# A transformer pair on one core: attention probabilities scaled on GpSimd before their transposes

## The reference, cut to what matters

```python
# first block: o_s and o_w, gated per head
p_s = jax.nn.softmax(jnp.where(dist_s >= 0, s_s, NEG_INF), axis=-1)
o_s = jnp.einsum('bgjtm,bgtmd->btgjd', p_s.astype(vsg.dtype), vsg)
...
o = g[..., 0:1] * o_c + g[..., 1:2] * o_s + g[..., 2:3] * o_w
# even layer
p = jax.nn.softmax(sc, axis=-1).astype(v.dtype)
return jnp.einsum('bkgqs,bskd->bqkgd', p, v)
...
oa = oa * jax.nn.silu(ga)
# odd layer
m = jnp.maximum(jnp.max(sc, axis=-1, keepdims=True), sink_l)
p = jnp.exp(sc - m)
denom = jnp.sum(p, axis=-1, keepdims=True) + jnp.exp(sink_l - m)
o = jnp.einsum('bnkgqs,bnskd->bnqkgd', (p / denom).astype(v.dtype), vb)
```

## Time and profile before

| | us |
|---|---|
| three runs | 1368.05, 1366.27, 1367.89 |
| median | 1367.89 |
| profiled execution | 1367.87 |
| its span, first to last instruction | 1365.3 |
| PE busy | 1316.9 (96%) |
| DVE busy | 820.5 (60%) |
| ACT busy | 440.2 (32%) |
| POOL busy | 637.6 (47%) |
| mean granted clock of PE | 0.987 |

### The profile page before, as it was taken

One profiled execution on the slowest core, in us unless ns is written; L12 is line 12 of the kernel. 1 busy time (PEld: TensorE's weight loads), 2 busy tenths in 40 slices (PEclk: granted clock), 3 DMA queues, 4 the chain that ended last, 5 costly groups with the idle time before them and its releaser, 6 DMA issues. The chain is left out here.

```text
span 1365.3 us, 19690 instructions
## 1 busy us (share of the span) xinstructions
PE 1316.9 (96%) x7254; PEld 1036.5 (76%) x7254; DVE 820.5 (60%) x1586; ACT 440.2 (32%) x948; POOL 637.6 (47%) x523
## 2 busy tenths in 40 slices
PE   7999999999999999999999999999999999999996
PEld 5897766688888888888788788876556788767675
DVE  4898689914554777777572456535655254156643
ACT  4201455523122112222110332255656122244521
POOL 5865222246676666666576365532000365622230
PEclk9999999999999999999999989999999999999998
DMA  5622110112343455555543124211000123211111
GB/s 177 239 68 77 32 41 24 46 62 83 103 169 123 169 187 200 199 186 191 178 155 95 44 93 152 88 47 32 0 1 1 62 83 93 93 38 41 32 47 62
DMA packets 37522, 130.24 MB, mean 95 GB/s; under 512 B 4544, under 2 KB 4800, under 8 KB 37184
## 3 DMA queue, kind: packets, MB, share of 16 engines
q1 hardware_dynamic: 26640, 93.11, 21.3%
q10 hardware_dynamic: 10800, 35.98, 7.1%
HBM read 126.98 MB, written 2.10 MB: 95 GB/s over the span
## 5 line engine op out<-in xcount | busy, mean ns | idle before, releaser
L1044 POOL TENSOR_TENSOR wlo<-raw,whi 128x1024 fp32r<-128x1024 f32 x171 | 417.0, 2438 | 14.3
L1040 POOL TENSOR_TENSOR whi<-raw,ones 128x2 fp32r<-128x2 f32 x171 | 40.9, 239 | 677.5 <-DMA raw<-in_w 677.5
L461 PE MATMUL bank<-ysplit,whi 128*128 128x512 f32 x984 | 314.5, 398 | 2.1 <-DVE xbuf L2254 2.1
L461 PE MATMUL bank<-hhi,whi 128*128 128x512 f32 x536 | 218.1, 407 | 0.4 <-DVE arena L2164 0.4
L461 PEld LDWEIGHTS bank<-ysplit,whi 128*128 128x128 f32 x984 | 184.4, 190 | 38.9 <-issue 3.2
L461 PE MATMUL bank<-hhi,wlo 128*128 128x512 f32 x536 | 209.9, 392 | 0.0
L461 PE MATMUL bank<-hlo,whi 128*128 128x512 f32 x536 | 209.4, 391 | 0.0
L461 PE MATMUL bank<-ysplit,wlo 128*128 128x512 f32 x496 | 194.9, 393 | 0.0
L1041 POOL TENSOR_SCALAR whi<-raw 128x1022 fp32r<-128x1022 f32 x171 | 185.8, 1086 | 0.0
L461 PEld LDWEIGHTS bank<-hhi,whi 128*128 128x128 f32 x536 | 100.9, 188 | 25.6 <-issue 6.6
L461 PEld LDWEIGHTS bank<-hhi,wlo 128*128 128x128 f32 x536 | 100.9, 188 | 22.0
(11 more groups left out here) (315 smaller groups left out, 2100.5 us busy)
## 6 DMA issues: line engine op xcount, KB each, us to landing
raw<-in_w SPq DMA_DIRECT2D x171, 512.0 KB, 3.6
arena<-in_ada ACTq DMA_DIRECT2D x48, 512.0 KB, 4.3
xbuf<-in_xT ACTq DMA_DIRECT2D x12, 256.0 KB, 5.6
xbuf<-in_w ACTq DMA_DIRECT2D x1, 2048.0 KB, 8.9
first<-in_w ACTq DMA_DIRECT2D x1, 2048.0 KB, 8.4
out_t<-xbuf SPq DMA_DIRECT2D x8, 256.0 KB, 2.2
xbuf<-in_xT SPq DMA_DIRECT2D x4, 256.0 KB, 6.4
first<-in_uq ACTq DMA_DIRECT2D x1, 768.0 KB, 6.5
```

What stands on the lines that cost most here:

```text
L461: m = mm(b[:, :], w[:, s, k * P:(k + 1) * P], x, start=(k == 0 and part == 0), stop=(k == DC - 1 and part == 2))
L1040: g.tensor_tensor(whi[:, s, 0:2], raw[:, s, 0:2], ones[:, :], ALU.mult)
L1044: g.tensor_tensor(wlo[:, s, :], raw[:, s, :], whi[:, s, :].bitcast(F32), ALU.subtract)\
```

## The change

Four things, in the words of the code:

1. Each step's two row sums are inverted at once by DVE (`inverse_sums`, one reciprocal of 128x2 per step). POOL multiplies the step's exps by them in place, half by half (`n_norm`, `ab_norm`, `c_norm`; in N by the gate as well), and PE's transposes wait for that (`p_norm`). All spreads are gone, with the multiplications by them. In N both branches of a head pair add up in one bank, and one addition per head pair takes it out with the compressed branch.
2. POOL's loop is written out: `splits` for whole stretches, and inside the attentions one part of a split (`split_part`: the high half, then two halves of the low one) behind a step's products.
3. In C the sink stands as one more column beside the scores (written by POOL, `c_sink`), so that the exp sums it; its own exp and sums are gone.
4. In AB and C ACT's copies of the transposes of step i-2 come ahead of the exps of step i. The down projection begins with banks 2, 3, 7 of its first two rows, and the wait for the modulation product stands ahead of bank 4; of the last four rows banks 0 and 1 of the first three come ahead of the wait for the last split. Even output units 3 to 7 use `EOUT_REST`.

```diff
@@ -178,7 +178,7 @@
...
-EOUT_BANKS = (0, 1, 2)
+EOUT_BANKS, EOUT_REST = (0, 1, 2), (3, 0, 1, 2)
...
@@ -352,13 +351,11 @@
...
-        p3 = area(3 * 2 * 3 * P).rearrange("p (s h n) -> p s h n", s=3, h=2)
+        p3 = area(3 * 2 * (3 * P + 1)).rearrange("p (s h n) -> p s h n", s=3, h=2)
...
@@ -572,7 +575,7 @@
...
-                    pe.wait_ge(*p_ready.at(("N", s, half)))
+                    pe.wait_ge(*p_norm.at(("N", s, half)))
...
@@ -582,26 +585,16 @@
...
-                if qt == 0:
-                    bank.take(pe, N_O, ("O", "N", s // TT))
-                b = bank.tiles[found[("bank", ("O", "N", s // TT))]]
+                if qt == 0 and br == 0:
+                    bank.take(pe, N_O, ("O", "N", i))
+                b = bank.tiles[found[("bank", ("O", "N", i))]]
...
                                vtok[:, kt, br * P + half * HD:br * P + half * HD + HD],
-                               npt[:, s % 2, half, kt * P:(kt + 1) * P], start=(kt == 0), stop=(kt == qt),
+                               npt[:, s % 2, half, kt * P:(kt + 1) * P], start=(br == 0 and qt == 0 and kt == 0), stop=(br == 1 and kt == qt),
...
-            def n_spread(p):
-                pe.wait_ge(*dve_did.at(("N", "rinv", p)))
-                b = bank.take(pe, C_R, ("N", "R", p))
-                for qt in range(TT):
-                    for half in range(2):
-                        x = n_col(p, half, qt)
-                        m = mm(b[64 * half:64 * half + 64, qt * P:(qt + 1) * P],
-                               rinv[:, x:x + 1].to_broadcast([P, HD]), ident[:, :], start=True, stop=True)
-                m.then_inc(*pe_did.up(("N", "R", p)))
...
@@ -762,17 +753,27 @@
...
-            pe.wait_ge(*dve_did.at(("ada", ADA_UP - 1)))
-            for i in range(FC):
-                u = UNIT[("down", i)]
-                pe.wait_ge(w_split.sem, u + 1)
+
+            def down_rows(i):
+                pe.wait_ge(w_split.sem, UNIT[("down", i)] + 1)
                 pe.wait_ge(*dve_did.at(("fa", i)))
-                for n in (2, 3, 6, 7, 4, 5, 1, 0) if i < LATE else ():
-                    if i == 0:
-                        bank.take(pe, (n,), ("down", n))
+
+            for part in (2, 3, 7), (6, 4, 5, 1, 0):
+                for i in range(2):
+                    down_rows(i)
+                    for n in part:
+                        if n == 4 and i == 0:
+                            pe.wait_ge(*dve_did.at(("ada", ADA_UP - 1)))
+                        if i == 0:
+                            bank.take(pe, (n,), ("down", n))
+                        m = down_block(i, n)
+                    if n == 0:
+                        m.then_inc(*unit_done.up(UNIT[("down", i)]))
+            for i in range(2, LATE):
+                down_rows(i)
+                for n in (2, 3, 7, 6, 4, 5, 1, 0):
                     m = down_block(i, n)
-                if i < LATE:
-                    m.then_inc(*unit_done.up(u))
+                m.then_inc(*unit_done.up(UNIT[("down", i)]))
...
@@ -784,8 +785,13 @@
...
+            for i in range(LATE, FC - 1):
+                down_rows(i)
+                for n in range(2):
+                    down_block(i, n)
+            down_rows(FC - 1)
             for n in range(DC):
-                for i in range(LATE, FC):
+                for i in range(LATE if n >= 2 else FC - 1, FC):
...
@@ -936,7 +930,7 @@
...
-                unit("eout", i, src=e_parts)
+                unit("eout", i, src=e_parts, pool=EOUT_REST)
...
@@ -1044,13 +1026,88 @@
...
+            def split_part(u, part):
+
+                s = u % WS
+                if part == 0:
+                    pool.wait_ge(landed[s].sem, u // WS * 16 + 16)
+                    g.tensor_tensor(whi[:, s, 0:2], raw[:, s, 0:2], ones[:, :], ALU.mult)
+                    g.tensor_scalar(whi[:, s, 2:D], raw[:, s, 2:D], 1.0, 1.0, ALU.mult, ALU.mult).then_inc(w_hi.sem, 1)
+                    return
+                at = slice((part - 1) * D // 2, part * D // 2)
+                pool.wait_ge(w_hi.sem, u + 1)
+                m = g.tensor_tensor(wlo[:, s, at], raw[:, s, at], whi[:, s, at].bitcast(F32), ALU.subtract)
+                if part == 2:
+                    m.then_inc(w_split.sem, 1)
...
+            def n_norm(s):
+                i, b, qt = n_steps[s]
+                L = (qt + 1) * P
+                pool.wait_ge(*dve_did.at(("N", "rinv", s)))
+                for half in range(2):
+                    x, gate = n_col(s // TT, half, qt), 3 * (i + 4 * half) + 1 + b
+                    g.tensor_scalar(np_[:, s % 3, half, 0:L], np_[:, s % 3, half, 0:L], rinv[:, x:x + 1],
+                                    gate3[:, qt, gate:gate + 1], ALU.mult, ALU.mult).then_inc(*p_norm.up(("N", s, half)))
...
+            def ab_norm(s):
+                p, qt = ab_steps[s]
+                pool.wait_ge(*dve_did.at(("AB", "rinv", s)))
+                for half in range(2):
+                    x = n_col(p, half, qt)
+                    g.tensor_scalar(abp[:, s % 3, half, :], abp[:, s % 3, half, :], rinv[:, x:x + 1], 1.0,
+                                    ALU.mult, ALU.mult).then_inc(*p_norm.up(("AB", s, half)))
...
+            first = UNIT[("q", 3)] + WS
+            splits(0, first)
+            pool.wait_ge(*dve_did.at(("qlo", 3)))
+            for i in range(len(n_steps)):
+                n_norm(i)
+                if i % TT:
+                    split_part(first + i // TT, i % TT - 1)
+            first, end = first + len(n_steps) // TT, UNIT[("ega", 2)] + WS
+            splits(first, end)
+            for i in range(len(ab_steps)):
+                ab_norm(i)
+                if 2 <= i < 20:
+                    split_part(end + (i - 2) // 3, (i - 2) % 3)
+            first, end = end + 6, UNIT[("og", 0)] + WS
+            splits(first, end)
+            pool.wait_ge(*dve_did.at("nsink"))
+            for i in range(3):
+                c_sink(i)
+            for i in range(len(c_steps)):
+                c_norm(i)
+                if i + 3 < len(c_steps):
+                    c_sink(i + 3)
+                if i % TT:
+                    split_part(end + i // TT, i % TT - 1)
+            splits(end + len(c_steps) // TT, NU)
...
@@ -1464,10 +1512,10 @@
...
+                if 2 <= i < n + 2:
+                    ab_copy(i - 2)
                 if i < n:
                     ab_exp(i)
-                if 2 <= i < n + 2:
-                    ab_copy(i - 2)
...
@@ -1506,16 +1554,16 @@
...
-                    A(p3[:, i % 3, half, 0:w], p3[:, i % 3, half, 0:w], ACT.Exp, bias=nmax[:, x:x + 1],
+                    act.wait_ge(*pool_did.at(("C", "sink", i)))
+                    A(p3c(i, half, 1), p3c(i, half, 1), ACT.Exp, bias=nmax[:, x:x + 1],
...
@@ -1531,15 +1579,10 @@
...
+                if 2 <= i < n + 2:
+                    c_copy(i - 2)
                 if i < n:
                     c_exp(i)
-                if 2 <= i < n + 2:
-                    c_copy(i - 2)
...
@@ -1834,28 +1877,18 @@
...
-            def n_rinv(p):
-                i, b = p // 2, p % 2
-                x = n_col(p, 0, 0)
-                dve.wait_ge(*p_ready.at(("N", p * TT + TT - 1, 1)))
-                link(V.reciprocal(rinv[:, x:x + 8], rsum[:, x:x + 8]))
-                r = rinv[:, x:x + 8].rearrange("p (t h) -> p t h", t=TT)
-                V.tensor_tensor(r, r, gate3[:, :, 3 * i + 1 + b:24:12], ALU.mult).then_inc(*dve_did.up(("N", "rinv", p)))
-
-            def n_out(p):
-                i, b = p // 2, p % 2
-                dve.wait_ge(*act_did.at(("N", "R", p)))
-                dve.wait_ge(*pv_done.at(("N", p * TT + TT - 1)))
-                dst = nacc(i) if b == 0 else hs[:, 0, :]
-                V.tensor_tensor(dst, bank.of(("O", "N", p))[:, :], nspread, ALU.mult).then_inc(*dve_did.up(("N", "t", p)))
-                bank.freed(("O", "N", p), dve_did, ("N", "t", p))
-                if b:
-                    dve.wait_ge(*dve_did.at(("N", "t", p)))
-                    link(V.tensor_tensor(nacc(i), nacc(i), hs[:, 0, :], ALU.add))
-
-            def n_add_cmp(i):
+            def inverse_sums(name, s, x):
+
+                dve.wait_ge(*p_ready.at((name, s, 1)))
+                V.reciprocal(rinv[:, x:x + 2], rsum[:, x:x + 2]).then_inc(*dve_did.up((name, "rinv", s)))
+
+            def n_out(i):
+
                 dve.wait_ge(*act_did.at(("cmp", "o", i)))
-                V.tensor_tensor(nacc(i), nacc(i), ncmp(i), ALU.add).then_inc(*dve_did.up(("N", "o", i)))
+                dve.wait_ge(*pv_done.at(("N", 8 * i + 7)))
+                V.tensor_tensor(nacc(i), bank.of(("O", "N", i))[:, :], ncmp(i), ALU.add)\
+                    .then_inc(*dve_did.up(("N", "o", i)))
...
@@ -2208,18 +2239,11 @@
...
-                dve.wait_ge(*pe_did.at(("AB", "R", p)))
                 dve.wait_ge(*dve_did.at(("g", "ega", p) if p < 4 else ("g", "egb", p - 4)))
-                if p:
-                    dve.wait_ge(*dve_did.at(("AB", "y", p - 1)))
```

(6 more changed lines are left out.)

134 lines of the change are left out of this document (44 added, 90 removed).

## The result

The changed kernel takes 1353.77 us (median of five runs, 1352.43 to 1357.61) against 1368.05 for the kernel before beside it; the ratio is 0.9897, with a 95% interval of 0.9879 to 0.9915. It is faster by 14 us where 24 were forecast: inside the range (1328 to 1363) and on the right side, but 10 us short of the likeliest value and just outside the forecast's own case (1336 to 1352). One of the five executions of the kernel before took 2616.91 us and is left out of the ratio. The profiled execution is the one of 1352.43 us, with a span of 1350.4.

The account below looks back on a forecast made before the run. PE was taken to bound the kernel nearly everywhere, DVE the second part of N. Terms N, AB, C, down stage, even outputs: 1367.9 + 6 - 12.5 - 6.0 - 8.7 - 2.9 = 1343.8 us; range 1328 to 1363.

Parts of the forecast that it names:

- N: First block's attention: -2 us in its first part, +8 in the second, where DVE sets the pace; +6 in all.
- C: Second block's third attention: -8.2 us for spreads (small PE products), +2 cover, -2.3 end, +2.5 start; -6.0 in all.
- AB: Second block's first two attentions: spreads give 7.8 us, most waits for ACT's copies go, products stay hidden; -12.5.
- the forecast's own case: Whole kernel: time falls within 1336 to 1352 us; chance 0.55.
- rival 3: N costs more: transposes wait for POOL's products too; +10 to +18 us there, total 1354 to 1362; chance 0.14.
- Down stage and even outputs: Down projection and even output units: new order and banks remove PE's gaps and slow clock; -8.7 and -2.9 us.
- Rival 4: Down stage: mended waits only move; 11.6 us of gains shrink to 2, total about 1354; chance 0.06.
- DVE reads PSUM in nearly all it does here: AB: step behind counting POOL's products as hidden, with 1.1 us to spare; the stage's forecast was -12.5 us.
- Who comes second waits to the end of the other's instruction: N: DVE's taps and POOL's instructions exclude each other; 20 pairs of products cost DVE 20 us.
- The waits at the end (2.1) go: End of C: the output no longer needs a spread; -2.3 us with the smaller waits beside them.
- Rival 1: N: products cost DVE nothing, so the stage follows PE; -12 us instead of +6, total 1326; chance 0.13.
- Rival 2: AB's bare steps and all N: pointer-scalar product costs 1.22 us (total 1361) to 1.5 (1380) for 512; chance 0.12.

## Why the prediction came out as it did

The time came out inside the range, but in part by luck: AB, C and C's start gave 12.3 us less than counted, and what hides it is the width of the range and 2.4 us less cost in N. Of the signs that were to show the forecast right, those of the down stage and of a product's price in AB came; those of N (PE idle before scores, taps over 0.95 us) and of AB (11 to 14 us shorter) did not, and PE waiting for POOL in N was the sign of rival 3.

- **Down stage and even outputs: right** (-8.7 and -2.9, measured -9.1 and -2.8). The gaps went, and with each the slow clock behind it. For the next stage's first unit in bank 0 the forecast had 0.8; 1.1 was measured. PE waits 0.9 of it, and DVE's residual (done at 1094.72) and POOL's split for that unit (done at 1094.80, the one that the profile names) end too close together to tell which of them it is. Rival 4 falls.
- **AB: the step that failed is "DVE reads PSUM in nearly all it does here", with the products counted as hidden.** The path through PE, POOL and ACT was worked out, and it held: the waits for products are 0.7 us in all. The price of a product was right too, 0.69 us for 512 columns (0.66 forecast). What was left out is DVE's small share of two-input work, the ropes, which the products stretch by 0.3 us each and the products with a part of a split behind them by 1.2, and what stands behind it: the maxima, and the scores. Size: 2.8 us, and about 1.3 for the slow clock that came with the gap of 2.0 us at 985 us (scores 2.41 us instead of 1.98, transposes 1.91 instead of 1.04). A second step failed with it: a spread covered this place, as it covered C's maxima. I looked for that cover in C and not in AB (1.8 us and 0.6 more of L850). The spreads themselves gave 0.87 us each on the path, 7.0 and not 7.8. The account: -7.0 - 5.5 (all of ACT's waits) + 4.6 + 0.6 + 0.7 + 1.3 = -5.3, measured -5.6. The run with ACT's old order shows the same from the other side: without it 0.8 is left of the 5.6.
- **N: right in sign, wrong in who pays.** The forecast let DVE pay: taps at a mean over 0.95 us, PE idle before scores. The taps are at 0.87 us, under the 0.92 of the earlier trace rows, and DVE has 16 us to spare. POOL pays, with products of 1.3 us instead of 0.34 to 0.66, and PE waits for them ahead of the transposes: the mechanism of rival 3, at a total of 2.0 us (3.6 with the echo below) in place of 10 to 18. Of the two parts, the first came out at +1.9 (I had counted -2, since PE was the bound there) and the second at +0.1 (+8). The step that failed is "Who comes second waits to the end of the other's instruction". A product that finds a tap at work lets the next tap go first as well: the first product at 212.77 lasts until 214.17 and has the whole tap of 213.26 to 214.01 in it, while the tap before it ended at 213.34. Of the 43 products in this part of N, 25 contain one whole tap and 3 contain two.
- **N's echo, +1.6**, was in no term. It is slow clock that sets in as the 32 one-column products of 288.5 us end; what brings it was not tested.
- **C: -8.5 forecast for the spreads, their cover and the end, -4.6 measured.** Per four steps 0.68 us came, as counted (1.0 less 0.3). Six such groups gave 4.1 us. The end, from the scores of step 28 on, is what failed: two spreads and the waits, together some 4.3 us, were to go, and 0.5 came. "The waits at the end (2.1) go" was taken for granted, and there PE waits 1.1 us for the copy (L981) and 1.9 for POOL's products (L963), where no filling is left. I had checked POOL's cover in AB's bare steps and not in C's, which are 2.2 to 2.8 us long and not 3.8. No run tests this end by itself.
- **C's start: right mechanism, too small.** 2.5 forecast, 4.0 measured. The 2.6 us between 1190.48 and 1193.1 were read rightly: PE waits 3.5, but it stood 0.73 there before too, so 2.8 are new. They had been put at 2, with some of the maxima hidden behind them, and none of it came back. The wait for ov 1's copy is 0.6 (0.5 forecast), and 0.6 of slow clock behind the gap was in no term.
- Rival 1 (the products cost DVE nothing in N) has its condition met, since the taps didn't get longer than before, but not its result: N took 3.6 us more and not 12 less. Rival 2 (a product of 1.22 us and more by itself) falls by the price, 0.69 and 0.77 us undisturbed for 512 columns, with one and two pointers. The Trainium skill's figure for 512 elements of a one-input loop (GPSIMD Engine Reference, section 3.1), 769 ns, is near both.

## What to carry to other kernels

Before work is put on POOL, list for every place which DVE instructions with two SBUF inputs will stand beside it, however few they are, what else POOL will do right behind it, and what is queued behind both; the price of the pair is decided by their order more than by their lengths. Release POOL's work where DVE goes over to reading PSUM: here one reciprocal moved ahead of the maxima was worth 10.6 us in N and AB, and the new normalisation with ACT's new order 6.6 in N, AB and C together, 4.8 of which hang on ACT's order in AB. When a change has several parts, run them apart before crediting the one in the title. When PE work is taken away, ask of each piece what it covered; and when a unit more or less draws from a rotation of banks, follow the rotation to its next stage.
